# Choosing the first expert's tokens before the rest of the routing in a two-layer transformer trunk

## The reference, cut to what matters

```python
def moe(h, router, w_gate_up, w_down):
    probs = jax.nn.softmax((xt @ router).astype(jnp.float32), axis=-1)
    top_p, top_i = lax.top_k(probs, TOP_K)                    # TOP_K = 2
    top_p = top_p / jnp.sum(top_p, axis=-1, keepdims=True)
    gates = jnp.sum(jax.nn.one_hot(top_i, N_EXPERTS) * top_p[..., None], axis=1)
    for e in range(N_EXPERTS):
        y = y + gates[:, e:e + 1] * swiglu(xt, w_gate_up[e], w_down[e])
```

## Time and profile before

| | us |
|---|---|
| median of 3 runs | 1138.62 |
| lowest and highest | 1137.79, 1139.30 |
| the profiled execution: its time | 1135.15 |
| its span in the trace | 1133.4 |
| PE busy | 1083.6 (96%) |
| DVE busy | 627.1 (55%) |
| ACT busy | 522.9 (46%) |
| DMA queue q1, share of 16 engines | 79.9% |

### The profile page before, as it was taken

How to read it: one execution, slowest core, us unless ns; L and a number is a source line. 1 busy time by engine, 2 the same in 40 slices (tenths; PEclk the granted TensorE clock), 3 DMA queues, 4 the chain that set the end, 5 groups by cost and what they waited for, 6 DMA issues and landing times.

```text
span 1133.4 us, 15880 instructions
## 1 busy us (share of the span) xinstructions
PE 1083.6 (96%) x5832; PEld 808.5 (71%) x5832; DVE 627.1 (55%) x712; ACT 522.9 (46%) x577; POOL 23.0 (2%) x94
## 2 busy tenths in 40 slices
PE   9998999999999999999998999998999999999994
PEld 9887888888898787787355787355787355787451
DVE  6866455555654458895116895106896106897102
ACT  6555444344445644774015774015775005776001
POOL 1100000000000000000000000000000000000000
PEclk9999999999999999999999999999999999999998
DMA  9933556555454424997999999999999999999994
GB/s 347 358 114 112 186 186 188 183 186 198 162 173 148 137 75 153 371 359 269 375 419 408 402 418 409 352 416 410 403 418 409 364 414 410 404 415 409 357 413 192
DMA packets 110935, 343.47 MB, mean 303 GB/s; under 512 B 11613, under 2 KB 38282, under 8 KB 100618
## 3 DMA queue, kind: packets, MB, share of 16 engines
q1 hardware_dynamic: 110714, 341.93, 79.9%
q10 hardware_dynamic: 144, 0.52, 0.1%
HBM read 341.37 MB, written 1.05 MB: 302 GB/s over the span
## 4 chain that ended last, share of the span: by engine, by line
PE 77%; DMA 7%; DVE 7%; ACT 3%; issue 2%; SPq 2%; POOL 0%; POOLq 0%; ACTq 0%; DVEq 0%
PE ps L1487 20%; PE ps L1482 18%; PE ps L1484 18%; PE ps L1483 18%; DMA raw<-moe_w_gate_up_dram 5%; DMA raw<-moe_w_down_dram 2%; SPq L368 2%; ACT whi L561 2%; DVE wlo L962 1%; PE ps L1827 1%; DVE wlo L949 1%; DVE wlo L951 1%; ACT xs L561 1%; DMA raw<-mla_w_down_dram 1%; DVE h L1144 1%
## 5 line engine op out<-in xcount | busy, mean ns | idle before, releaser
L561 ACT ACTIVATE whi<-raw 128x2048 fp32r<-128x2048 f32 (+2 forms) x203 | 341.7, 1688 | 245.8 <-PE ps L1484 226.8
L962 DVE TENSOR_TENSOR wlo<-raw,whi 128x2048 fp32r<-128x2048 f32 x151 | 345.7, 2294 | 119.5 <-ACT whi L561 118.3
L1482 PE MATMUL ps<-whi,xhi 128*128 128x512 f32 (+3 forms) x688 | 264.3, 384 | 16.3 <-DVE wlo L962 9.2
L1484 PE MATMUL ps<-wlo,xhi 128*128 128x512 f32 (+3 forms) x688 | 260.2, 378 | 0.0
L1483 PE MATMUL ps<-whi,xlo 128*128 128x512 f32 (+3 forms) x688 | 259.7, 377 | 0.0
L1482 PEld LDWEIGHTS ps<-whi,xhi 128*128 128x128 f32 x688 | 129.9, 189 | 45.2 <-DVE wlo L962 8.5
L1487 PE MATMUL ps<-raw,xs 128*64 128x512 f32 (+2 forms) x1024 | 155.0, 461 | 0.0
L1484 PEld LDWEIGHTS ps<-wlo,xhi 128*128 128x128 f32 x688 | 129.6, 188 | 23.9
L1483 PEld LDWEIGHTS ps<-whi,xlo 128*128 128x128 f32 x688 | 129.8, 189 | 22.5
L1487 PEld LDWEIGHTS ps<-raw,xs 128*64 128x64 f32 x1024 | 68.2, 137 | 81.7 <-issue 71.5
L1482 PE MATMUL ps<-whi,hhi 128*128 128x512 f32 x264 | 105.9, 401 | 0.0
(11 more groups left out here) (299 smaller groups left out, 972.3 us busy)
## 6 DMA issues: line engine op xcount, KB each, us to landing
raw<-moe_w_gate_up_dram SPq DMA_DIRECT2D x256, 512.0 KB, 12.7
raw<-moe_w_down_dram SPq DMA_DIRECT2D x80, 1024.0 KB, 17.1
raw<-moe_w_gate_up_dram SPq DMA_DIRECT2D x96, 384.0 KB, 9.4
raw<-ffn_w_gate_up_dram SPq DMA_DIRECT2D x44, 512.0 KB, 4.9
raw<-ffn_w_down_dram SPq DMA_DIRECT2D x22, 512.0 KB, 4.3
raw<-kv_shared_w_dram SPq DMA_DIRECT2D x16, 512.0 KB, 4.2
raw<-moe_w_gate_up_dram SPq DMA_DIRECT2D x32, 256.0 KB, 9.6
raw<-moe_w_down_dram SPq DMA_DIRECT2D x16, 512.0 KB, 17.7
```

The lines of the kernel that those rows point to most:

```text
L561: return nc.scalar.activation(o, i, ACT.Copy, scale=scale)
L962: V.tensor_tensor(wlo[:, s, :].rearrange("p a w -> p (a w)"), raw[:, (hh // 2) % RAW, :], whi[:, s, :].bitcast(F32).rearrange("p a w -> p ...
L1482: pe.matmul(o, a_hi, b_hi, start=start, stop=False, skip_group_check=True)
L1484: return pe.matmul(o, a_hi, b_lo, start=False, stop=stop, skip_group_check=True)
```

## The change

The tokens of expert 0 no longer wait for the full choice. A token takes expert 0 when fewer than two of its logits are larger than logit 0, so DVE compares the logits with logit 0, adds up, and compares with 1.5 (`first_msk`); PE makes the places from that one column (three products instead of five) and DVE writes `sel` from them. The second `pick`, `msk` and the places of all experts come after, and on DVE the low parts of the gathered tokens (`gathered_low(0)`) now stand ahead of the copy of the places and of everything that makes the tables. The sums of squares come before the copies of the transposes, ACT and DVE copy half of these each, and ACT alone writes both halves of `xm`. The fillers are fewer: none between the router's products (2 before), 3 instead of 12 after them, 5 instead of 4 ahead of the gather, none instead of 9 behind it.

```diff
@@ ACT
-            for b in range(3):
+            act.wait_ge(h_ready[3], 4)
+            squares(3, 0, xm[:, 0, :])
+            for b in range(2):
                 act.wait_ge(x_tr[3], b + 1)
                 copy(xr[:, 2 * b:2 * b + 2, :], ps[:, X_BANKS[3][b], :].rearrange("p (a s) -> p a s", a=2)).then_inc(xhi_ready[3], 1)
-            squares(3, 0, xm[:, 0, :])
+            act.wait_ge(ss_ready[3], 2)
             act.wait_ge(rstd_ready[3], 1)
-            act.wait_ge(ss_ready[3], 2)
-            copy(xm[:, 1, :], h[:, 1, :], scale=rstd[:, 3, 1:2]).then_inc(xm_ready, 1)
+            for c in range(TC):
+                copy(xm[:, c, :], h[:, c, :], scale=rstd[:, 3, c:c + 1]).then_inc(xm_ready, 1)
@@ DVE
-            dve.wait_ge(x_tr[3], 4)
-            V.tensor_copy(xr[:, 6:8, :], ps[:, X_BANKS[3][3], :].rearrange("p (a s) -> p a s", a=2)).then_inc(xlo_ready[3], 1)
+            dve.wait_ge(h_ready[3], 4)
             squares(3, 1, xm[:, 1, :])
-            dve.wait_ge(rstd_ready[3], 1)
-            dve.wait_ge(ss_ready[3], 2)
-            V.tensor_scalar(xm[:, 0, :], h[:, 0, :], rstd[:, 3, 0:1], None, ALU.mult).then_inc(xm_ready, 1)
-
+            for b in range(2, 4):
+                dve.wait_ge(x_tr[3], b + 1)
+                V.tensor_copy(xr[:, 2 * b:2 * b + 2, :], ps[:, X_BANKS[3][b], :].rearrange("p (a s) -> p a s", a=2)).then_inc(xlo_ready[3], 1)
...
+            step(V.tensor_tensor(sc8[:, :, :], lg[:, :, :], lg[:, :, 0:1].to_broadcast([P, TC, N_EXP]), ALU.is_gt))
+            step(V.tensor_reduce(better[:, :], sc8[:, :, :], AX, ALU.add))
+            V.tensor_scalar(first_msk[:, :], better[:, :], 1.5, None, ALU.is_lt).then_inc(first_ready, 1)
+
             pick(lg[:, :, :], m1[:, :], oh1[:, :, :])
+            dve.wait_ge(first_placed, 1)
+            step(V.tensor_copy(first_pos[:, :], ps[:, 5, 40:40 + TC]))
+            for c in range(TC):
+                V.tensor_scalar(sel[:, c, :], iota[:, :], first_pos[:, c:c + 1], first_msk[:, c:c + 1],
+                                ALU.is_equal, ALU.mult).then_inc(sel_ready, 1)
...
+            dve.wait_ge(rstd_ready[3], 1)
             V.tensor_tensor(best[:, :], best[:, :], rstd[:, 3, :], ALU.mult).then_inc(gap_ready, 1)
+            gathered_low(0)
             dve.wait_ge(pos_done, 1)
             step(V.tensor_copy(posn[:, :, :].rearrange("p c e -> p (c e)"), ps[:, 5, 16:32]))
-
-            for c in range(TC):
-                V.tensor_scalar(sel[:, c, :], iota[:, :], posn[:, c, 0:1], msk[:, c, 0:1],
-                                ALU.is_equal, ALU.mult).then_inc(sel_ready, 1)
...
             V.tensor_scalar(final_i[:, :], extra[:, 2:3], float(PAIRS - 1), None, ALU.add).then_inc(items_ready, 1)
-            gathered_low(0)
             split_low(H_SBO + RING + 7)
@@ PE
-            keep_clock(12, 4)
+            keep_clock(3, 4)
+            pe.wait_ge(first_ready, 1)
+            mm(ps[:, 5, 40:41], before[:, :], first_msk[:, 0:1], False, True)
+            mm(ps[:, 5, 41:42], ones[:, :], first_msk[:, 0:1], False, False)
+            mm(ps[:, 5, 41:42], before[:, :], first_msk[:, 1:2], False, True).then_inc(first_placed, 1)
+            keep_clock(5, 4)
+            pe.wait_ge(xm_ready, 2)
+            gather(0)
             pe.wait_ge(msk_ready, 1)
...
-            keep_clock(4, 4)
-            pe.wait_ge(xm_ready, 2)
-            gather(0)
-            keep_clock(9, 4)
             begin("big", 0, 0)
```

More of the change, by code:

```diff
@@ L216, in build @@
         lg, lg2, oh1, oh2, sc8, msk, gates, posn, posc, ovf, csum, key, place, cap, cap2, wide, csum2, extra, less, order, oh, prod, \
-            m1, m2, den, best, rank, cnt, tf, xr = over(
+            m1, better, first_msk, first_pos, m2, den, best, rank, cnt, tf, xr = over(
                 *[(f"rt_{n}", [P, TC, N_EXP], F32) for n in
@@ L222, in build @@
                 ("rt_oh", [P, ITEMS, N_EXP], F32), ("rt_prod", [P, ITEMS, N_EXP], F32),
-                ("rt_m1", [P, TC], F32), ("rt_m2", [P, TC], F32),
+                ("rt_m1", [P, TC], F32), ("rt_better", [P, TC], F32), ("rt_first_msk", [P, TC], F32), ("rt_first_pos", [P, TC], F32), ("rt_m2", [P, TC], F32),
                 ("rt_den", [P, TC], F32), ("rt_best", [P, TC], F32), ("rt_rank", [P, N_EXP], F32),
@@ L275, in build @@
         lg_done, gap_ready, gap_exp = (sem(n) for n in ("lg_done", "gap_ready", "gap_exp"))
+        first_ready, first_placed = sem("first_ready"), sem("first_placed")
         msk_ready, pos_done, items_ready = sem("msk_ready"), sem("pos_done"), sem("items_ready")
@@ L1981, in _ @@
             for k in range(KD):
-                if k in (2, 4):
-                    keep_clock(1, 4)
-                if k < 6:
+                if k < 4:
                     pe.wait_ge(xhi_ready[3], k // 2 + 1)
                 else:
-                    pe.wait_ge(xlo_ready[3], 1)
+                    pe.wait_ge(xlo_ready[3], k // 2 - 1)
                 for c in range(TC):
```

## The result

| | before | after |
|---|---|---|
| median of 7 runs each, same chip | 1138.57 | 1143.59 |
| lowest and highest | 1136.46, 1139.86 | 1140.27, 1144.75 |
| the profiled execution: its time | 1135.15 | 1143.69 |
| its span in the trace | 1133.4 | 1140.4 |

The ratio is 1.0040, with a 95% interval of 1.0027 to 1.0054: 3.1 to 6.1 us slower. The prediction had the sign, but its 1141.0 and the top of its range, 1143.0, were too low. The medians differ by 5.0 us, 2.6 more than the forecast's 2.4. The traces differ by 7.0 us of span, since the profiled run of before was 3.4 us under its median.

The account below looks back on a forecast made before the run. DVE's list up to unit 4 was taken to bound the kernel. +0.23 +0.52 +0.21 -1.11 +1.8 +0.76, with roundings, gave +2.43 on 1138.62: 1141.0 us; own range 1140.3 to 1142.0, 8 in 10 from 1138.8 to 1143.0.

Parts of the forecast that it names:

- What bounds the kernel: From the routing on, DVE's instruction list sets unit 4; a shift there moves the end nearly one to one.
- Rival C: Weight stream carries the first item, so its slack swallows the lateness: no change, 1138.6 us; 12%.
- Logits: Router stretch up to DVE's copy of the logits: 0.23 us later, at 421.44.
- minus of 0.60 for the fillers: Within the logits' step: dropping two fillers between the router's products saves 0.30 us each.
- Count: DVE between logits' copy and first pick: three more instructions, +0.52 us.
- Places of expert 0: PE's six records take 0.86 us, DVE doesn't wait; second copy +0.21, old idle 1.11 goes.
- Gather: PE's gather of the tokens starts at 424.17, 2.04 us sooner; the five fillers ahead cost nothing.
- Low parts: DVE's low parts of the gathered tokens wait for ACT, about 1.8 and 0.76 us.
- Rest of DVE: DVE's list behind the low parts: unit 2's half at 436.42, end of unit 4 at 448.18, 2.43 us later.
- PE: PE starts unit 0 3.4 us sooner, then stalls some 3, 3 and 2 us ahead of units 2, 3, 4.
- Rival A: Clock falls in PE's new stalls; costs only if it reaches unit 4, up to +1.7 us, 1142.8; 20%.

Follow-up runs that it names:

- e9: Before with no filler at all from the router's first product to unit 0; 1138.17 us against 1137.76 for before.
- i3: Before with unit 2's half made in the wait for the places, gathered low parts halved among table work, later tables spread out, nine fillers gone; 1133.64 us, ratio 0.9968.
- e6: After's early selection with before's squares, copies, scaled tokens and router fillers; 1140.50 us against 1136.89 for before.
- e11: e6 with the tables spread as in i3 and unit 2's half ahead of the gathered low parts; 1138.15 us against 1137.76 for before.
- e2: Before without its two fillers between the router's products; 1136.84 us against 1137.05 for before.
- e1: After with before's two fillers put back between the router's products; 1143.53 us against 1137.05 for before.
- e3: After with more 128-column fillers ahead of, among and behind the router's products; 1143.85 us against 1137.05 for before.
- e5: After with 512-column fillers in the routing in place of the narrow ones; 1142.46 us against 1136.89 for before.
- e8: Before with fewer, 512-column fillers in place of its 128-column ones; 1137.16 us against 1137.25 for before.

## Why the prediction was right or wrong

**What bounds the kernel: right.** DVE's list sets unit 4 in after too (445.21 and 449.55 in the chain), and no slack takes the lateness back in the traces: unit 4 is 6.98 us later behind the residual add, the start of the chain's long DMA piece 6.6 (595.39 - 412.73 against 589.70 - 413.63), the end of the span 7.9. Rival C is out. SP's longest wait, for the same half, grew from 23.8 to 30.8:

```profile
SPq L369 <- DVE wlo L952: 30.8, 1, 30.8
```

***Logits*: wrong, +2.44 instead of +0.23.** The pieces on ACT and DVE came as said: squares, then two copies, and PE's wait of 0.57 for the first. What failed is the assumption that the router's products keep their 0.96 us for eight records. They took 5.78 us for 32, against 3.64 at the upper level in e9; the 2.14 between them is nearly all of the 2.21 that the step is off. The minus of 0.60 for the fillers held: without the 2.14 the copy would be at 7.88, forecast 7.81.

***Count*: right in kind.** From the logits' copy to the first pick there are 0.70 us (423.45 - 422.75), less the 0.2 that the pick was behind the copy anyway: 0.5 for 0.52.

***Places of expert 0*: wrong.** From their start to DVE's copy the six records took 425.38 - 423.99 = 1.39 instead of 0.86, and the three fillers ahead of them, which the step passed over, took 1.42: `first_msk` was ready at 423.55, PE at 423.99. DVE waited 0.93 where the forecast had no wait.

***Gather*: wrong.** It is 2.09 later, not 2.04 sooner. "The five fillers end at the same time as `sel`" held only at the upper level: here the gather started at 427.40 behind them, 1.2 us after `sel` (425.57 + 0.60 = 426.17). No run took after's fillers out altogether, so what they cost there at the low clock is read from this one trace.

***Low parts*: the mechanism right, the size off.** DVE waits for ACT ahead of the first and the fifth low part, 3.35 and 0.66 us instead of 1.8 and 0.76. The first carries the slow gather, 2.54 us from its start to ACT's `xhi` instead of 2.06:

```profile
429.94 1.14 ACT L562 ACTIVATE xhi<-ps,gcol 128x128 fp32r<-128x128 f32 x4 [1.93 <-PE ps L1494]
```

***Rest of DVE* and *PE*: right.** 20.78 us for 20.77. PE stalls ahead of units 2, 3 and 4 as said, 2.84, 1.58 and 1.35 us instead of about 3, 3 and 2; unit 2 at half clock filled part of the second.

**Rival A had the right cause in the wrong place.** I looked for the clock in new idle time of PE and found the fall there, hidden. (The 1.7 us that the prediction gave to one fall was its low time times the missing clock, not a lateness that a trace showed.) The one that cost came while PE was busy. The falls in the routing of after and e9 are equally long, 10.2 us, with 5.1 us of full clock missing in each; in after 4.58 arrived, as measured against the forecast, in e9 1.15, against before. The Trainium skill, "TensorE: Matmul & The Clock Gate", section Terms, prices slow time at that time times (1 - K/N); after's trace comes near it, e9's doesn't. What decides is whether PE has work at that time, and what waits for it. Why the clock falls there, and whether it must with the new order, stays open.

**The base was weak too.** The forecast priced PE from a trace in which the clock never left 1.00 in the routing. The time of that execution, 3.5 us under the median, was a sign that others differ, and it was read as an offset. If most runs of before lose time to a fall, that is why the medians miss the forecast by 2.6 us and the traces by 4.6; no trace shows it.

**The range.** "The forecast's own range (1140.3 to 1142.0)" doesn't follow from its bounds: +1.9 and +3.0 on 1138.62 give 1140.5 to 1141.6, and with the 0.8 of the runs 1139.7 to 1142.4. The measured 1143.59 is outside either.

## What to carry to other kernels

Before you take work from between a producer on PE and its consumer, ask what that work was hiding: in before and e9, 6 us of tables covered a gather at either clock, and after's low parts waited for every slow product. Thin out the consumer's list first (i3, 3.6 us); starting the producer sooner was worth nothing in either order that I ran (e6 against before, e11 against i3). And where a profiled run is faster than the median, don't price TensorE's products from it alone: e2, nearly the same kernel, had a fall of the clock in its routing that before's profile lacks.

## What the hardware showed that I hadn't expected

- The granted clock fell to 0.50 and stayed there for 9 us with PE busy all the time (10.00 of 10.00 us from 418 to 428 in after). Ahead of it PE did sixteen transposes of 128 columns and was idle for 0.27 and 0.57 us; in it were products of 8 and of 1 columns and fillers of 128. It was back at 1.00 some 1.1 us into the gather, in e9 about 4.
- Fillers hold it unreliably. With those of 128 columns the fall came 2 to 3 us later (e1, e3); with those of 512 there was none in the routing in e5, and one in e8. An fp32 filler of 512 columns took 0.9 us at 2.4 GHz.
- Where PE was busy, the whole of the missing clock showed in its products, whatever their width. The gather took 5.81 us in e9 against 3.81, 2.00 more, and the clock was low for its first 4.2 us, 2.1 missing. Six records of 512 columns took 2.82 us in e5 at the upper level and 4.52 in e8, 1.70 more, with 3.4 us of low clock, 1.7 missing:

```profile
420.63 4.52 PE L1487 MATMUL ps<-h,ident 128*128 128x512 f32 x6
```
